# A hybrid attention, convolution and MoE block: 512-column matmuls for a whole head turn, a start in quarters, one expert loop and four stores

## The reference, cut to what matters

```python
h = rms_norm(x, g_mix)                                   # x: 256 x 1024
proj = h @ w_in + b_in                                   # 6656 columns: q k v cb cc cx ga gc
y_attn = sliding_window_attention(rope(q), rope(k), v, sinks) @ w_attn_o
y_conv = (cb * causal_short_conv(cc * cx, w_conv)) @ w_conv_o
merged = sigmoid(ga) * y_attn + sigmoid(gc) * y_conv
x = x + merged @ w_out
x = x + moe_ffn(rms_norm(x, g_ffn))                      # 32 experts, top 4, clamped SwiGLU
return rms_norm(x, g_final)
```

## Time and profile before

| | us or share |
|---|---|
| median of three executions | 1176.75 |
| profiled execution | 1176.24 |
| its span, first to last instruction | 1174.5 |
| PE (TensorE) busy | 1119.5 (95%) |
| VectorE busy | 346.8 (30%) |
| ScalarE busy | 228.4 (19%) |
| bytes moved by DMA | 447.62 MB, mean 381 GB/s |

### The profile page before, as it was taken

One profiled execution on the slowest core, in us unless ns is written; L12 is line 12 of the kernel. 1 busy time (PEld: TensorE's weight loads), 2 busy tenths in 40 slices (PEclk: granted clock), 3 DMA queues, 4 the chain that ended last, 5 costly groups with the idle time before them and its releaser, 6 DMA issues.

```text
span 1174.5 us, 14862 instructions
## 1 busy us (share of the span) xinstructions
PE 1119.5 (95%) x5876; PEld 531.6 (45%) x5876; DVE 346.8 (30%) x660; ACT 228.4 (19%) x401; POOL 40.6 (3%) x60
## 2 busy tenths in 40 slices
PE   8999999999999999999999999999999999999996
PEld 7999998973333333333333333333333333333332
DVE  6977786741111211211111111111111111111111
ACT  5666665421000110010010000010000000000002
POOL 4101100000000000000000000000000000000000
PEclk9999999999999999999999999999999999999999
DMA  9554748899999999999999999999999999999995
GB/s 289 160 166 150 263 167 316 294 398 414 428 428 428 428 427 427 427 426 429 429 429 429 428 427 428 427 428 427 427 427 429 427 429 428 429 429 429 427 425 222
DMA packets 72699, 447.62 MB, mean 381 GB/s; under 512 B 5721, under 2 KB 46005, under 8 KB 47189
## 3 DMA queue, kind: packets, MB, share of 16 engines
q1 hardware_dynamic: 72240, 446.67, 92.4%
q10 hardware_dynamic: 421, 0.38, 0.1%
HBM read 445.59 MB, written 1.05 MB: 380 GB/s over the span
## 4 chain that ended last, share of the span: by engine, by line
PE 62%; DMA 36%; ACT 0%; SPq 0%; issue 0%; ACTq 0%; DVE 0%; DVEq 0%
DMA ring<-in_w_up 32%; PE psum L768 30%; PE psum L486 6%; PE psum L500 5%; PE psum L719 4%; PE psum L781 4%; DMA ring<-in_w_down 3%; PE psum L490 3%; PE psum L520 2%; PE psum L504 2%; PE psum L794 1%; PE psum L727 1%; DMA params<-in_g_ffn 0%; PE psum L741 0%; PE psum L788 0%; PE psum L559 0%
## 5 line engine op out<-in xcount | busy, mean ns | idle before, releaser
L768 PE MATMUL psum<-ring,work 128*64 128x512 f32 x3072 | 689.6, 595 | 38.7 <-DMA ring<-in_w_up 36.5
L768 PEld LDWEIGHTS psum<-ring,work 128*64 128x64 f32 x3072 | 212.4, 137 | 466.0 <-issue 376.8
L1440 DVE TENSOR_SCALAR work<-psum 128x512 f32<-128x512 f32 x32 | 22.1, 692 | 284.0 <-PE psum L768 284.0
L1201 DVE TENSOR_TENSOR w<-ring,w 128x1024 fp32r<-128x1024 f32 x70 | 82.9, 1226 | 13.2 <-ACT w L957 12.7
L1445 DVE TENSOR_SCALAR work<-psum 128x512 f32<-128x512 f32 x32 | 22.1, 692 | 205.4 <-PE psum L768 205.4
L957 ACT CAST w<-ring 128x1024 fp32r<-128x1024 f32 x74 | 74.2, 1048 | 29.4 <-PE psum L490 15.8
L1100 ACT COPY work<-psum 128x512 f32<-128x512 f32 x32 | 18.8, 587 | 311.0 <-PE psum L794 310.9
L1463 DVE TENSOR_TENSOR work<-psum,g2k 128x256 f32<-128x256 f32 x62 | 23.4, 419 | 166.8 <-PE psum L727 166.8
L486 PE MATMUL psum<-hh,w 128*128 128x256 f32 x512 | 67.3, 284 | 0.0
L781 PE MATMUL psum<-work 64*128 64x512 f32 x256 | 63.6, 615 | 1.4 <-ACT work L1105 1.4
L1109 ACT ACTIVATE work<-work 128x512 f32<-128x512 f32 x32 | 20.2, 630 | 228.9 <-DVE work L1440 228.9
(11 more groups left out here) (202 smaller groups left out, 769.1 us busy)
## 6 DMA issues: line engine op xcount, KB each, us to landing
ring<-in_w_gate SPq DMA_DIRECT2D x63, 2048.0 KB, 44.9
ring<-in_w_up SPq DMA_DIRECT2D x63, 2048.0 KB, 42.0
ring<-in_w_down SPq DMA_DIRECT2D x58, 2048.0 KB, 43.3
ring<-in_w_in SPq DMA_DIRECT2D x26, 1024.0 KB, 5.0
ring<-in_w_down SPq DMA_DIRECT2D x11, 1024.0 KB, 35.7
ring<-in_w_conv_o SPq DMA_DIRECT2D x4, 1024.0 KB, 5.8
ring<-in_w_attn_o SPq DMA_DIRECT2D x4, 1024.0 KB, 6.1
ring<-in_w_out SPq DMA_DIRECT2D x4, 1024.0 KB, 8.6
```

The source lines that it names most:

```text
L768: mm = pe.matmul(psum[64 * h:64 * h + 64, b, :], src[:, k, :], w[:, k2, h * 512:(h + 1) * 512], start=(bias_of is None and k == 0), stop=( ...
L1201: v.tensor_tensor(wL[:, par, m, :, :], slot(s).rearrange("p (k n) -> p k n", k=KB)[:, :, m * P:(m + 1) * P], wH[:, par, m, :, :].bitcast(F ...
```

## The change

It has five parts. (1) At the start x is normalized in quarters of 256 columns, each transposed as it is there; the first column block k=0 is transposed into bank 0 of its own; g_mix comes in a DMA of its own ahead of the others and is transposed alone, the other 84 parameter rows later; the first piece comes in two DMAs of 512 KiB (four k each) and its high part is cast in these halves by VectorE; `WARM` goes from 4 to 3 and `KEEP_WARM` from 2 to 1; GpSimd splits only the first piece. (2) In a head turn cx, cb, ga and gc also go by `project_both`, each into two banks; ScalarE takes their low columns out with the bias (`take_low`), VectorE adds the high columns, and the sigmoids run over both halves at once in place. PE waits for `u_ready` before ga (was: before gc), for `z_ready` before gc (was: at the turn's end), and for `sums_ready` before cc and at the turn's end. (3) `spread_down_bias` moves from expert 16 to expert 4. (4) PE's experts 5 to 29 run in one loop. (5) SyncE makes all four stores, one for each row tile and half.

```diff
-WARM, KEEP_WARM = 4, 2
+WARM, KEEP_WARM = 3, 1
 PAIRS = ((4, 5), (0, 1), (2, 3))
 Q_BANKS, C_BANKS = (2, 3), (0, 6)
+X_BANKS, B_BANKS, GA_BANKS, GC_BANKS = (1, 2), (0, 6), (1, 2), (0, 7)
...
-            load1(0, w_in[:, :, KCOL * PW:(KCOL + 1) * PW])
+            for half, full in enumerate((first_in, piece_full[0])):
+                ks = slice(4 * half, 4 * half + 4)
+                sp.dma_start(slot(0).rearrange("p (k n) -> p k n", k=KB)[:, ks],
+                             w_in[:, ks, KCOL * PW:(KCOL + 1) * PW]).then_inc(full, 16)
...
-            for t in range(TT):
-                h0 = (0, 512)[t]
-                if t == 0:
-                    sp.wait_ge(out_ready[t][0], 1)
-                sp.wait_ge(out_ready[t][1], 1)
-                sp.dma_start(out[0, t * P:(t + 1) * P, h0:D], normed[:, t, h0:D]).then_inc(out_done, 16)
-            sp.wait_ge(out_done, 16 * 3)
+            for t, h in ((0, 0), (0, 1), (1, 1), (1, 0)):
+                sp.wait_ge(out_ready[t][h], 1)
+                at = slice(h * 512, (h + 1) * 512)
+                sp.dma_start(out[0, t * P:(t + 1) * P, at], normed[:, t, at]).then_inc(out_done, 16)
+            sp.wait_ge(out_done, 16 * 4)
...
-                    pe.wait_ge(normed_ready, t + 1)
                     for k in range(KB):
-                        tr = pe.transpose(bank(3 + k // 2, (k % 2) * T + t * P, P), normed[:, t, k * P:(k + 1) * P], ident)
-                        if t == TT - 1 and k % 2:
+                        if k % 2 == 0:
+                            pe.wait_ge(normed_ready, 4 * t + k // 2 + 1)
+                        tr = pe.transpose(turned(k)[:, t * P:(t + 1) * P], normed[:, t, k * P:(k + 1) * P], ident)
+                        if t == TT - 1 and (k == 0 or k % 2):
                             tr.then_inc(done, 1)
...
+                    if k % 4 == 0:
+                        pe.wait_ge(first_high, k // 4 + 1)
                     for m in range(2):
-                        if k == 0:
-                            pe.wait_ge(first_high, m + 1)
...
-            pe.wait_ge(par_in, 64)
-            pe.transpose(bank(7, 0, 92), params[:, :], ident[0:92, 0:92]).then_inc(par_turned, 1)
+            pe.wait_ge(mix_in, 16)
+            pe.transpose(bank(7, 0, 8), mix_rows, ident[0:8, 0:8]).then_inc(par_turned, 1)
             turn_normed(x_turned)
+            pe.wait_ge(par_in, 48)
+            pe.transpose(bank(2, 0, 84), params[:, :], ident[0:84, 0:84]).then_inc(par_turned, 1)
...
                 project_both(Q_BANKS, i * 6 + 2, 0, hh)
+                pe.wait_ge(sums_ready, i * 2 + 1)
                 project_both(C_BANKS, i * 6 + 3, 1, hh, lambda: pe.wait_ge(bank6_read, i + 1))
...
-                project_T(1, i * 6 + 4, 0, (hH, hL), scores)
-                pe.wait_ge(raw_ready, i + 2)
-                project_T(2, i * 6 + 5, 1, (hH, hL))
+                def scores_and_raw():
+                    scores()
+                    pe.wait_ge(raw_ready, i + 2)
+
+                project_both(X_BANKS, i * 6 + 4, 0, hh, scores_and_raw)
                 pe.wait_ge(cc_ready, i + 1)
-                project_T(0, i * 6 + 6, 0, (hH, hL))
+                project_both(B_BANKS, i * 6 + 5, 1, hh)
+                pe.wait_ge(u_ready, i + 1)
+                project_both(GA_BANKS, i * 6 + 6, 0, hh)
...
-                pe.wait_ge(u_ready, i + 1)
-                project_T(1, i * 6 + 7, 1, (hH, hL))
+                pe.wait_ge(z_ready, i + 1)
+                project_both(GC_BANKS, i * 6 + 7, 1, hh)
...
-                pe.wait_ge(z_ready, i + 1)
-                pe.wait_ge(gates_ready, i * 2 + 2)
+                pe.wait_ge(sums_ready, i * 2 + 2)
...
-                if at(j, MID * UNROLL + 1):
+                if at(j, UNROLL - 1):
...
-            with pe.Fori(1, MID) as it:
-                group(it)
-            group(MID)
-            with pe.Fori(MID + 1, NE // UNROLL) as it:
+            with pe.Fori(1, NE // UNROLL) as it:
                 group(it)
...
+            def take_low(i, nth, banks, col, to):
+
+                for b in range(2):
+                    act_e.wait_ge(blocks_done, i * 12 + (9 + 2 * nth + b))
+                    nc.scalar.activation(to[b], psum[:, banks[b], T:2 * T], ACT.Identity,
+                                         bias=bT[:, bass.ds(i * 2 + (2 * col + b), 1)]).then_inc(part_low, 1)
+
+            def gate_rows(which, i):
+                return [which[:, bass.ds(i * 2 + b, 1), :].rearrange("p a t -> p (a t)") for b in range(2)]
+
+            def open_gate(i, nth, which):
+
+                act_e.wait_ge(sums_ready, i * 2 + nth + 1)
+                gate = which.rearrange("p (i m) t -> p i (m t)", m=2)[:, bass.ds(i, 1), :]
+                nc.scalar.activation(gate, gate, ACT.Sigmoid).then_inc(gates_ready, 1)
...
+                take_low(i, 0, X_BANKS, CX, [u[:, b, 2:T + 2] for b in range(2)])
...
+                act_e.wait_ge(rotated, i + 2)
+                take_low(i, 1, B_BANKS, CB, [swp[:, b, :] for b in range(2)])
                 act_e.wait_ge(z_ready, i + 1)
                 nc.scalar.copy(zH[:, bass.ds(i * 2, 2), :], ycv).then_inc(zH_ready, 1)
-                for which, b, col, due in ((ga, 0, GA, 7), (gc, 1, GC, 8)):
-                    act_e.wait_ge(blocks_done, i * 12 + 2 * due)
-                    for m in range(2):
-                        ins = nc.scalar.activation(which[:, bass.ds(i * 2 + m, 1), :].rearrange("p a t -> p (a t)"),
-                                                   psum[:, b, m * T:(m + 1) * T], ACT.Sigmoid,
-                                                   bias=bT[:, bass.ds(i * 2 + (2 * col + m), 1)])
-                    ins.then_inc(gates_ready, 1)
-                    if which is ga:
-                        split_high_in_turn(i, 6)
-                        act_e.wait_ge(pT_turned, i + 1)
-                        nc.scalar.copy(pT[:, 0:4, :].rearrange("p n q -> p (n q)"), psum[:, 3, :]).then_inc(pT_ready, 1)
-                        nc.scalar.copy(pT[:, 4:12, :].rearrange("p n q -> p (n q)"),
-                                       psum[:, 4:6, :].rearrange("p b n -> p (b n)")).then_inc(pT_ready, 1)
+                take_low(i, 2, GA_BANKS, GA, gate_rows(ga, i))
+                act_e.wait_ge(pT_turned, i + 1)
+                nc.scalar.copy(pT[:, 0:4, :].rearrange("p n q -> p (n q)"), psum[:, 3, :]).then_inc(pT_ready, 1)
+                nc.scalar.copy(pT[:, 4:12, :].rearrange("p n q -> p (n q)"),
+                               psum[:, 4:6, :].rearrange("p b n -> p (b n)")).then_inc(pT_ready, 1)
+                split_high_in_turn(i, 6)
+                open_gate(i, 1, ga)
+                take_low(i, 3, GC_BANKS, GC, gate_rows(gc, i))
                 act_e.wait_ge(o_ready, i + 1)
                 nc.scalar.copy(aH[:, bass.ds(i * 2, 2), :].rearrange("p m t -> p (m t)"),
                                psum[:, 6, :]).then_inc(aH_ready, 1)
+                open_gate(i, 2, gc)
...
+            def first_weights(half):
+
+                ks = slice(4 * half, 4 * half + 4)
+                dve.wait_ge((first_in, piece_full[0])[half], 16)
+                v.tensor_copy(wH[:, 0, :, ks, :].rearrange("p m k n -> p k m n"),
+                              slot(0).rearrange("p (k m n) -> p k m n", k=KB, m=2)[:, ks]).then_inc(first_high, 1)
...
+                for quarter in range(4):
+                    at = slice(quarter * PW, (quarter + 1) * PW)
+                    v.tensor_scalar(normed[:, t, at], xres[:, t, at], small[:, 4 + t:5 + t], None, ALU.mult).then_inc(normed_ready, 1)
+                    if t == 0 and quarter == 1:
+                        mean_rows_in(1)
...
+                if k == 2:
+                    first_weights(1)
+                dve.wait_ge(hH_ready, k + 1 if k < 2 else 2 * (k // 2) + 2)
...
+                dve.wait_ge(part_low, i * 8 + 2)
+                steps.link(v.tensor_tensor(u[:, :, 2:T + 2], psum[:, X_BANKS[0]:X_BANKS[1] + 1, 0:T], u[:, :, 2:T + 2], ALU.add))
+                v.tensor_tensor(u[:, :, 2:T + 2], u[:, :, 2:T + 2], ccs, ALU.mult).then_inc(u_ready, 1)
...
+                dve.wait_ge(part_low, i * 8 + 4)
                 for b in range(2):
-                    ins = v.scalar_tensor_tensor(ycv[:, b, :],
-                                                 psum[:, 2, b * T:(b + 1) * T], bT[:, bass.ds(i * 2 + (2 * CB + b), 1)],
-                                                 ycv[:, b, :], ALU.add, ALU.mult)
-                ins.then_inc(z_ready, 1)
+                    ins = v.tensor_tensor(swp[:, b, :], psum[:, B_BANKS[b], 0:T], swp[:, b, :], ALU.add)
+                steps.link(ins)
+                v.tensor_tensor(ycv, swp, ycv, ALU.mult).then_inc(z_ready, 1)
                 split_low_in_turn(i, 5)
+                dve.wait_ge(blocks_done, i * 12 + 14)
+                dve.wait_ge(part_low, i * 8 + 6)
+                gate = ga[:, bass.ds(i * 2, 2), :]
```

(23 more changed lines are left out.)

75 lines of the change are left out of this document (32 added, 43 removed).

## The result

The changed kernel takes 1168.61 us, the median of four executions (1167.83 to 1169.12), beside 1176.92 for the kernel before (1176.15 to 1177.34, also four): a ratio of 0.9931, with a 95% interval from 0.9919 to 0.9944. That is 8.3 us less. Over the 15 to 21 executions of the kernel before that stand beside each group of experiments its median is 1176.2 to 1176.4, and the gain by them 7.7. The forecast was 4.4 less, 1172.3 with a range down to 1170.4: the direction was right, and the size was half of what came.

The account below looks back on a forecast made before the run. PE was taken to bound the mixer and the expert weights' DMA the rest. Gains of 1.2 (start), 2.7 (head turns), 0 (experts) and 0.5 (end) summed to 4.4 us, giving a median of 1172.3, range 1170.4 to 1176.3.

Parts of the forecast that it names:

- The bounds: Whole kernel: PE paces the mixer, the expert weights the rest; a mixer ending earlier starts the full stream as much earlier.
- Rival D: Experts: the weight stream doesn't follow the mixer, whose gain ends as waiting; only the end gains, 1176.2 us; chance 7%.
- The start: Up to the first piece's end: quartered normalization and earlier transposes and casts gain 1.2 us, bounds 0.9 and 1.5.
- The halved first load: First piece in two DMAs: same sum unless the second half landed after 10.75 us, despite the 1 MiB batching rule.
- The head turns: Mixer's four turns: fewer matmuls for the same columns, 32 halves at 0.085 us, gain 2.7; bound below 1.5.
- The waits: PE's new or earlier waits in a head turn: no stall, 0.7 us left at p_ready, 0.5 at z_ready.
- The experts: Expert stretch: moving spread_down_bias and using one loop each gain zero, 0.3 us either way.
- The end: Output stores after the last normalizations: four stores gain 0.5 us, bounds 0 and 0.9.
- its completion stays: Last store: issued 1 us earlier, yet completing as before, while the transfer starts 0.8 us earlier.
- A: Head turns: ScalarE loads two more tables a turn; 1178.9 us at 1.8 a load, 1175.9 at 1.28; chance 7%.
- B: Head turns: VectorE is late, PE waits, turns stay at 39.1 us and the 2.7 are gone, 1175.0; chance 14%.
- C: Start: with fewer dummies PE's clock falls to 1.2 GHz and the first piece's time doubles, 1176.1 us; chance 8%.

Follow-up runs that it names:

- experiment 6: The kernel after with PE's wait on z_ready at a head turn's end put back beside the new one: 1168.64 us.
- experiment 8: The kernel after with PE's four head turns written out in place of their loop: 1170.02 us, ratio 0.9946.
- experiment 1: The kernel before with only spread_down_bias moved, from expert 16 to expert 4: 1176.31 us, ratio 0.9998.
- experiment 5: Three store runs: before with SyncE's four stores, 1176.43 us; after with its last store on ScalarE, 1168.74; before with ScalarE's store moved to SyncE, 1176.33.
- experiment 4: The kernel after with before's loops, bias place and stores, so only start and head turns changed: 1171.36 us, ratio 0.9954.
- experiment 2: The kernel before with spread_down_bias at expert 4 and PE's experts 5 to 29 in one loop: 1174.26 us, ratio 0.9982.
- e3: The kernel after with all six groups of PE's experts written out, no loop: 1172.51 us, ratio 0.996.
- e13: The kernel after with PE's program lengthened by 17 activation turns in a branch not executed, 5393 instructions for 5257: 1170.21 us, ratio 0.9947.

## Why the prediction was right and where it was wrong

**The bounds: right.** PE set the pace of the mixer and the weights that of the rest, and 4.7 us less in the mixer were 4.7 us less at the first expert. Rival D is out.

**The start: right.** Forecast 1.2, measured 1.30 in the two profiled executions, and 1.17 between the medians of all kernels with the old start (17.85, six of them) and with the new one (16.68, eight). The steps came near: the last quarter at 9.12 for 9.3, the low part of the first piece at 14.69 for 14.7. The second row tile was taken up at 7.98, for 8.2 in the working. The halved first load did no harm: its second half was cast from 10.43 on, ahead of the 10.75 at which it would have begun to cost. "DMA: Bandwidth & Descriptors" of the Trainium skill, the throughput table's rule, wants transfers batched to 1 MiB; no run here shows a price for halving this one, since nobody waited for it.

**The head turns: the mechanism right, the term too small.** Forecast 2.7, measured 3.36. The halves cost 2.79 for 2.88, as taken, 0.7 in a turn. What the working left out is the joint between two turns: 0.17 us of issue and a first group of 2.11 that is now 2.04, together some 0.2 in a turn, though the turns as a whole gained 0.84 and not 0.9. It is not the count of waits (experiment 6) and not the loop's end, which is there in the kernel after and gone in experiment 8, at the same length. What it was stays open. The waits held as worked out: 0.7 left at `p_ready` (forecast 0.7), 0.66 at `z_ready` (forecast 0.5). VectorE is at 87% (forecast 85%) and ScalarE at 26.4 us (forecast 27.3).

**The experts: the step that failed.** "One loop for a loop, a group and a loop changes no instruction that is executed. Zero for both": the first sentence is true and the second doesn't follow. PE's program is itself moved by DMA, 16.4 kB at a time, and where a queue that never empties sets the pace, what holds up one of its engines delays it. Eleven packets less at 0.15 to 0.2 us are 1.7 to 2.2, and all eleven are missing between 520 and 1140 us (12 before, 1 after). Ten are two groups of program text, the one that was written out and the body of the second loop, at five packets each; one goes because the mixer's program is shorter. The trace of the two kernels has 1138.32 - 1133.03 - 3.36 = 1.9. The row "q8 instruction: 31" stood on the page of before, and I read the DMA share as weights alone. It would have given the count, not the price: by bytes alone eleven packets are 0.4 us. That `spread_down_bias` costs nothing was right (experiment 1).

**The end: the stores right, the border missed.** Forecast 0.5 with bounds 0 and 0.9, measured 1.9. The four stores give 0.65 to 0.7 in the traces, too little for the times of experiment 5 to show. The working had "its completion stays" and 0.8 from an earlier start, which is near. The other 1.2 of the 1.9 come from the border of PE's program, which lay among the last stores before and lies elsewhere since the program is shorter. It goes with the program's length, whichever edit changes that. The working had read the 2.27 us of the two issues in the earlier trace rows as what stores take; 1.4 of them went with the packet.

**Sum.** Start 1.3, turns 3.4, program 1.9, stores 0.7, border 1.2: 8.5, the difference of the spans (1174.5 - 1166.0). The parts done alone agree: mixer 5.1 (experiment 4, of which about 1.2 is the border, which the changed mixer moved too: 30.55 blocks), loop 2.1 (experiment 2). For the mixer 4.7 + 1.2 would be 5.9; the interval of that run's ratio, 3.8 to 6.9 us, takes it in.

**The rivals.** A: two table loads of 1.28 in a turn, before L1019 and L985, none between a sigmoid and the Identity passes of gc. That agrees with "ScalarE: Activation LUTs" of the Trainium skill, which has Identity in every table set; its 2.66 for a switch with its drain isn't borne out, as the sigmoid starts at 97.03, at the end of the load from 95.74. B: 0.66 and 0.7 us were left, so thin is true and late is not. C: the first piece ran at the upper level, even without dummies. But what stood against C, that PE idled before the transposes and the clock held, is misread: eight dummies kept PE busy from 2.63 to 7.86 in the kernel before, and its first record of the granted clock is at 5.74. The range failed on its lower side because none of the rivals said that the kernel could gain more than the sum of its parts: all four took something away.

No version in these runs beats the changed kernel. One with the groups of experts in the loop from the first on would have fewer packets still; it wasn't tried, since the first two experts differ from the others.

## What to carry to other kernels

Where transfers set the pace, everything that the DMA moves is in the sum, the program too: read the row of the instruction packets, see in which stretch they lie, and put long straight code into loops there, or into a stage where the queue has room. "Executes the same instructions" is no reason for a zero. When a kernel changes length, look at whether the last packet of its program has moved into or out of the last stores before giving that microsecond to an edit, and give the forecast a rival that gains more, as well as those that gain less.

## What the runs showed of the hardware

- PE's program comes by DMA during the execution, in packets of 16.4 kB, as many as 256 instructions of PE's program go into it (30.55 blocks: 30 packets; 40.40: 40). The body of the experts' loop, five packets long, is fetched once and not again in its later turns (12, 0 and 1 packets in three stretches). Whether a longer body would be isn't shown.
- A packet costs 0.15 to 0.2 us where the stream is full and nothing that can be measured at a share of 0.50. It holds up one of the sixteen parts of a load by 1.5 us (32 us for 21 packets in e3), and the load is complete with its slowest part.
- A packet among the last stores costs 0.8 to 1.9 us. In six kernels of seven one store's issue then takes 1.2 to 1.95 us for 0.34 to 0.46; in e13 it leaves a hole of 1.25 us in which 8 to 25 GB/s are moved.
- PE starts at the lower level of its clock: transposes 0.213 us apart and the first record at 10.76 without dummies, 0.111 apart and the first record at 6.20 with them. A window before the first record says 1.00 all the same.
